# HGRN2 pair scores: two half-width products per tile against one full-width product on keys that ScalarE mixes, in a two-layer diffusion trunk

## The reference, cut to what matters

```python
def step(s, inp):                       # one chunk, one direction
    qc, kc, vc, lfc = inp
    cum = jnp.cumsum(lfc, axis=1)
    dec = jnp.exp(jnp.where(causal, cum[:, :, None] - cum[:, None], -jnp.inf))
    scores = jnp.sum(qc[:, :, None] * kc[:, None] * dec, axis=-1)
    o = jnp.einsum('btsh,bshv->bthv', scores, vc)
    o = o + jnp.einsum('bthk,bhkv->bthv', qc * jnp.exp(cum), s)
    ...
o_cf, s_cf = _hgrn2_chunkwise(q_c, kf_c, i_c, lf_c, s0)
o_lf, _ = _hgrn2_chunkwise(q_l, kf_l, i_l, lf_l, s_cf)
o_cb, s_cb = _hgrn2_chunkwise(rev(q_c), rev(kb_c), rev(i_c), rev(lb_c), s0)
o_lb, _ = _hgrn2_chunkwise(rev(q_l), rev(kb_l), rev(i_l), rev(lb_l), s_cb)
```

## Time and profile before

| | |
|---|---|
| Runs | 1993.79, 1994.34, 1997.75 us; median 1994.34 |
| The profiled execution | 1995.78 us; span 1994.0 us (its first to its last instruction), so 1.8 us lie outside the span |
| Busy, of the span | PE 1825.0 us (92%), DVE 1170.0 (59%), ACT 342.2 (17%), POOL 72.9 (4%) |
| Levels stage of layer 0 | about 346.1 to 434.6 us |
| Levels stage of layer 1 | about 1144.1 to 1196.4 us |
| Mean granted TensorE clock | 0.955 of 2.4 GHz |

### The profile page before, as it was taken

One profiled execution on the slowest core, in us unless ns is written; L12 is line 12 of the kernel. 1 busy time (PEld: TensorE's weight loads), 2 busy tenths in 40 slices (PEclk: granted clock), 3 DMA queues, 4 the chain that ended last, 5 costly groups with the idle time before them and its releaser, 6 DMA issues.

```text
span 1994.0 us, 34547 instructions
## 1 busy us (share of the span) xinstructions
PE 1825.0 (92%) x15227; PEld 1167.8 (59%) x15227; DVE 1170.0 (59%) x1387; ACT 342.2 (17%) x613; POOL 72.9 (4%) x60
## 2 busy tenths in 40 slices
PE   4999999986799999998999987699999999999997
PEld 1334556874344434344546665486877868677694
DVE  2021166783533222313223594599999999999996
ACT  2001054002422221212012403200000000100100
POOL 0023000000000000000050000000000000000000
PEclk9999999997899999999999997799999999999999
DMA  9631100001345544321212003399999999999999
GB/s 331 265 156 64 62 23 21 23 1 43 116 180 211 183 155 173 123 105 43 84 63 85 17 27 155 120 371 381 401 402 410 405 410 404 404 411 406 410 408 380
DMA packets 114980, 420.42 MB, mean 211 GB/s; under 512 B 14008, under 2 KB 20856, under 8 KB 108688
## 3 DMA queue, kind: packets, MB, share of 16 engines
q1 hardware_dynamic: 112784, 417.13, 53.8%
q10 hardware_dynamic: 2048, 1.02, 0.2%
HBM read 417.08 MB, written 1.05 MB: 210 GB/s over the span
## 4 chain that ended last, share of the span: by engine, by line
PE 78%; DVE 12%; issue 3%; DMA 3%; ACT 2%; DVEq 1%; POOLq 0%; SPq 0%; PEldq 0%; ACTq 0%; POOL 0%; PEld 0%
PE PS L1303 11%; PE PS L610 11%; PE PS L608 8%; PE PS L1590 6%; PE PS L1592 6%; PE PS L1593 6%; DVE ARENA L1708 6%; PE PS L1263 6%; PE PS L1612 5%; PE PS L1198 3%; PE PS L828 3%; PE PS L444 2%; PE PS L1091 2%; DMA ARENA<-in_ada_w 1%; PE PS L1570 1%
## 5 line engine op out<-in xcount | busy, mean ns | idle before, releaser
L1708 DVE TENSOR_TENSOR ARENA<-ARENA 128x2816 bf16<-128x2816 f32 (+1 forms) x192 | 584.1, 3085 | 21.6 <-DMA ARENA<-in_moe_w 19.7
L1590 PE MATMUL PS<-ARENA 128*128 128x96 bf16 x2816 | 377.2, 209 | 27.9 <-DVE ARENA L1708 15.8
L1593 PE MATMUL PS<-ARENA 128*128 128x96 bf16 x2816 | 376.7, 209 | 4.0 <-issue 4.0
L1592 PE MATMUL PS<-ARENA 128*128 128x96 bf16 x2816 | 376.9, 209 | 3.2 <-issue 3.1
L1590 PEld LDWEIGHTS PS<-ARENA 128*128 128x128 bf16 x2816 | 281.2, 100 | 39.3 <-issue 21.4
L1592 PEld LDWEIGHTS PS<-ARENA 128*128 128x128 bf16 x2816 | 281.2, 100 | 7.3 <-issue 7.2
L1593 PEld LDWEIGHTS PS<-ARENA 128*128 128x128 bf16 x2816 | 281.3, 100 | 4.1 <-issue 4.0
L610 PE MATMUL PS<-ARENA 128*128 128x512 f32 (+1 forms) x608 | 244.4, 542 | 2.3 <-ACTq L394 2.3
L1303 PE MATMUL PS<-ARENA 128*128 128x512 bf16 x1056 | 236.0, 384 | 2.4 <-DVE ARENA L1334 2.4
L1612 PE MATMUL PS<-ARENA 128*96 128x512 bf16 x1056 | 237.3, 384 | 0.0
L377 DVE TENSOR_TENSOR ARENA<-ARENA 128x4096 bf16<-128x4096 f32 (+1 forms) x26 | 91.4, 3522 | 201.9 <-ACT ARENA L371 201.9
(11 more groups left out here) (221 smaller groups left out, 1573.5 us busy)
## 6 DMA issues: line engine op xcount, KB each, us to landing
ARENA<-in_moe_w SPq DMA_DIRECT2D x136, 1408.0 KB, 11.4
ARENA<-in_moe_w SPq DMA_DIRECT2D x48, 1536.0 KB, 14.6
ARENA<-in_ada_w SPq DMA_DIRECT2D x24, 2048.0 KB, 9.6
ARENA<-in_ffn_w SPq DMA_DIRECT2D x15, 2048.0 KB, 7.6
ARENA<-in_w_in SPq DMA_DIRECT2D x12, 2048.0 KB, 8.0
ARENA<-in_moe_w SPq DMA_DIRECT2D x16, 1024.0 KB, 15.9
ARENA<-in_w_out SPq DMA_DIRECT2D x8, 1024.0 KB, 5.4
ARENA<-in_w_in SPq DMA_DIRECT2D x4, 1024.0 KB, 6.2
```

Of the source, the lines that this page charges most:

```text
L1590: pe.matmul(out, hi[:, f:f + P], HEH[:, k, :], start=k == 0 and b % 4 == 0, stop=False, skip_group_check=True)
L1592: pe.matmul(out, hi[:, f:f + P], HEL[:, k, :], start=False, stop=False, skip_group_check=True)
L1593: mm = pe.matmul(out, lo[:, f:f + P], HEH[:, k, :], start=False, stop=k == KC - 1, skip_group_check=True)
L1708: dve.tensor_tensor(WLO[q % NSLOT][:, 0:n], RAW[q % NSLOT][:, 0:n], WHI[q % NSLOT][:, 0:n], ALU.subtract).then_inc(S("m_lo"), 1)
```

## The change

`KE[d]` isn't the stationary matrix of a level any more. ScalarE copies the early half of each block from `KE[0]` and the late half from `KE[1]` into a new view `KEX` (two copies per pair and level, `act_cross_keys`), and PE makes one product per head and tile: `KEX` stationary, 128 query columns moving, into 128 columns of PSUM. The moving columns come from both query views: early-half queries from `QP[1]`, late-half queries from `QP[0]`. One access pattern with four dimensions reads them in the order of the tokens (`crossed_queries`); for it, the two query views change places, so that the step from `QP[1]` to `QP[0]` is positive. `KEX` lies at KiB 116 to 124, which nothing else uses in this stage. PE waits for both copies of its pair and level (semaphore `h{p}_keys`). A copy of level n >= 1 waits until PE is through with level n-1 of the pair (the old `KEX` has been read) and until DVE has ended the update of its direction. ScalarE's fetches of the output gate, which stood alone in its queue, now stand between the copies. The updates, the takes, the masks, level -1 and the products of the gate projection are as before.

```diff
--- before.py
+++ after.py
@@ -177,10 +177,11 @@
 
         ST = A(100, NH, 512)
         Q = A(16, NH, 512)
-        QP = [A(24, NH, 512), A(32, NH, 512)]
+        QP = [A(32, NH, 512), A(24, NH, 512)]
         KE = [A(40, NH, 512), A(48, NH, 512)]
         FG = [A(56, NH, 512), A(64, NH, 512)]
         TB = [A(108, 1024), A(112, 1024)]
+        KEX = A(116, NH, 512)
         SST = A(56, 3, 2, NH, P)
         KDT = A(68, 2, NH, P)
         V = A(72, NT, 512)
@@ -232,7 +233,7 @@
             "t_act": 4, "t_dve": 3, "dp_x": NT, "o_gated": 2 * NT,
             "o_added": 2 * NT, "out_mm": 2 * NT}
         for p in range(2):
-            in_layer0.update({f"h{p}_mm": 1 + len(LEVELS), f"h{p}_taken": 1 + len(LEVELS)})
+            in_layer0.update({f"h{p}_mm": 1 + len(LEVELS), f"h{p}_taken": 1 + len(LEVELS), f"h{p}_keys": 2 * len(LEVELS)})
             for d in range(2):
                 in_layer0.update({f"h{d}{p}_qp": 1, f"h{d}{p}_upd": 3 * len(LEVELS)})
         for step in ("s", "mx", "nb", "exp", "r", "ratio", "p", "pt", "at", "pv", "o"):
@@ -793,6 +794,28 @@
             new = totals(n_level + 1).rearrange("p (g b) -> p g b", g=2)
             eng.tensor_tensor(new, tv[:, :, :, 0], tv[:, :, :, 1], ALU.mult).then_inc(S(n + "upd"), 1)
 
+        SIDE = NH * 512
+
+        def crossed_queries(h, x, m):
+
+            a = 256 * 24 + 512 * h + P * x
+            v = ARENA[:, a:a + 2 * (SIDE + m)].rearrange("p (g w) -> p g w", g=2)[:, :, 0:P]
+            return v.rearrange("p g (b two m) -> p b g two m", two=2, m=m)[:, :, :, 0, :]
+
+        def act_cross_keys(act, L, n_level, p):
+
+            a, m = first_query(L), LEVELS[n_level]
+            if n_level:
+                act.wait_ge(S(f"h{p}_mm"), since(L, f"h{p}_mm") + n_level + 1)
+            for d in range(2):
+                if n_level:
+                    act.wait_ge(S(f"h{d}{p}_upd"), since(L, f"h{d}{p}_upd") + 3 * n_level)
+
+                def halves(v):
+                    return v[:, PAIRS[p], a:].rearrange("p g (b h m) -> p g b h m", h=2, m=m)[:, :, :, d, :]
+
+                act.activation(halves(KEX), halves(KE[d]), ACT.Copy).then_inc(S(f"h{p}_keys"), 1)
+
         def level_bank(n_level, p):
 
             return 2 * ((2 * (n_level + 1) + p) % 3)
@@ -808,6 +831,7 @@
                                 pe.wait_ge(S(n + "qp"), since(L, n + "qp") + 1)
                             else:
                                 pe.wait_ge(S(n + "upd"), since(L, n + "upd") + 3 * n_level)
+                        pe.wait_ge(S(f"h{p}_keys"), since(L, f"h{p}_keys") + 2 * n_level + 2)
                     at = 2 * (n_level + 1) + p
                     if at >= 3:
                         pe.wait_ge(S(f"h{1 - p}_taken"), since(L, f"h{1 - p}_taken") + (at - 3) // 2 + 1)
@@ -819,20 +843,22 @@
                                 pe.matmul(bank[:, c], KE[0][:, h, c], Q[:, h, c], start=True, stop=False)
                                 mm = pe.matmul(bank[:, c], KE[1][:, h, c], Q[:, h, c], start=False, stop=True)
                                 continue
-                            for d in range(2):
-                                late = 1 - d
-
-                                def halves(v):
-                                    return v.rearrange("p (b h m) -> p b h m", h=2, m=LEVELS[n_level])[:, :, late, :]
-
-                                mm = pe.matmul(halves(bank[:, c]), KE[d][:, h, c], halves(QP[d][:, h, c]), start=True, stop=True)
+                            mm = pe.matmul(bank[:, c], KEX[:, h, c], crossed_queries(h, x, LEVELS[n_level]), start=True, stop=True)
                     mm.then_inc(S(f"h{p}_mm"), 1)
                     w = KC * gate_units(L)
                     for step in range(w * at // 16, w * (at + 1) // 16):
                         pe_proj_fill(pe, L, KC * NT + step)
 
         def act_levels(act, L):
-            for j in range(gate_units(L)):
+            taken = 0
+            for n_level in range(len(LEVELS)):
+                for p in range(2):
+                    act_cross_keys(act, L, n_level, p)
+                    done = KC * gate_units(L) * (2 * n_level + p + 1) // 16 // KC
+                    while taken < done:
+                        act_proj_one(act, L, FIRST + NT + taken)
+                        taken += 1
+            for j in range(taken, gate_units(L)):
                 act_proj_one(act, L, FIRST + NT + j)
 
         def dve_take(dve, L, p, n_level):
```

## The result

| | before | changed |
|---|---|---|
| Median of the runs | 1994.07 us (8 runs) | 1998.91 us (8 runs) |
| Profiled execution | 1995.78 us | 2002.08 us |

What follows compares the result with a forecast made beforehand. The prediction took PE as the bound in layer 0's levels stage and DVE in layer 1's. Gains of 14.8 and 0.9 us, with copies costing 0, gave 1994.34 - 15.7 = 1978.6 us, range 1974.5 to 1984.5.

Steps and rivals of the forecast that it cites:

- Nothing else is moved: Outside the two levels stages: everything behind them, the expert stage included, only comes 15.7 us earlier.
- Bounds: Levels stages: PE bounds layer 0 at 5.29 us per position; DVE bounds layer 1, hiding PE's time.
- Term 1: New products in the levels stages: 0.110 us per record, so 1.76 us per layer 0 position instead of 3.52.
- the two ends given: Cost of a new product record with the crossed read: low bound 0.110 us, high bound 0.221 us.
- Term 2: DVE becomes layer 0's bound; its vanishing waits for products gain 14.8 us there and 0.9 us in layer 1.
- Term 3: ScalarE's new copies: 0.63 us each in layer 0, about 0.42 in layer 1, hidden, costing 0.
- 2.6 us to spare: Layer 0, pair 0: copy and products ready at 5.7 us of a level's 8.3, when DVE asks.
- Rival A: Level 0 alone dear: crossed read costs 0.221 us per record there; gain 11.7 us, total 1982.6 us; chance 0.08.
- B: Crossed read costs double at every level, positions as long as before; no gain, 1994.3 us; chance 0.04.
- D: Copies late at 3.5 times the estimate, ScalarE the bound; 4.2 us of gain lost, 1982.8 us; chance 0.04.
- C: Levels stages: PE's clock falls to half; 25 us lost in layer 0, about 8 in layer 1; 2027 us; chance 0.04.

Runs made afterwards that it cites:

- run 4: Changed kernel with 134 more met-wait instructions on PE and level 0's moving columns read from one query view, not crossed: 1979.49 us, ratio 0.9930 to the kernel before.
- run 8: Changed kernel with 134 more met-wait instructions on PE and each ScalarE copy made twice: 1982.34 us, ratio 0.9948 to the kernel before.
- run 1: Changed kernel with 134 more met-wait instructions on PE ahead of its first matmul: 1982.60 us, ratio 0.9932 to the kernel before.
- run 6: Changed kernel with PE's loop over the eight experts written out, no padding, other engines still looping: 1974.19 us, ratio 0.9897 to the kernel before.
- run 9: Changed kernel with 100 more met-wait instructions on PE ahead of its first matmul: 2027.48 us, ratio 1.0165 to the kernel before.
- run 3: Changed kernel with 60 more met-wait instructions on PE ahead of its first matmul: 2018.39 us, ratio 1.0121 to the kernel before.

## Why the prediction was wrong, step by step

- **"Nothing else is moved ... The expert stage, long as it is, starts from the end of layer 1's states and only shifts"** is the step that failed. What was moved was the code itself: 646 instructions fewer on PE ahead of a loop, so the loop's first instructions lie elsewhere in the pieces in which they are fetched. That gave back 19.4 us, more than the change had gained. The order listing had the count before the forecast was made (32 places fewer in each position of layer 0), and the page of the kernel before had the queue (q8, "instruction"); what was missing was to look at the stop at the branch in the loop and ask what it hangs on.
- Bounds (PE in layer 0, DVE in layer 1): right. The chain names DVE in layer 0 now.
- Term 1, the pace of the new products: 0.112 to 0.125 us from level 1 on in layer 0 and 0.12 to 0.13 in layer 1, but 0.166 at level 0, half way between the two ends given. Level 0 costs 1.4 us in layer 0 and 0.4 in layer 1 (run 4).
- Term 2, what DVE lets through: 14.8 + 0.9 forecast, 14.1 + 0.4 measured; the difference is mostly the dear level 0.
- Term 3, the copies: 0.65 and 0.42 us instead of 0.63 and 0.42; they cost nothing (run 8). PE does wait for them, 5.6 us in layer 0, which the sum with its 2.6 us to spare didn't have, but it has time for that.
- Rival A had the right mechanism at half its price: DVE's first wait stayed at 3.2 us instead of 4.0, the second at 0.4 instead of 1.3. B and D did not happen. C, the slower case, was about the clock: it stayed at 1.00 and 0.99 in the two stages. The kernel got slower for a reason that none of the rivals had.
- With the loop back at its old place the changed kernel takes 1982.6 us (run 1), 4.0 above the forecast and inside its range. Of these, 1.2 are the two stages' shortfall; the expert stage adds 0.8, the rest lies in the scatter of medians. That it is rival A's 1982.6 to the digit is chance: the two stages got 14.5 us shorter, not A's 11.7.

## What to carry to other kernels

When a change alters how many instructions an engine has ahead of a long loop, the loop's own time can change with it, by up to 45 us here for the same work, in a cycle of 256 instructions. Before an edit is judged by its total, compare the stages it doesn't touch; if one of them differs, with "issue" gaps at the same instruction of each pass, shift the loop with a few met waits and measure again. Where a loop on the bounding engine has few passes, writing it out removes the question.

## What the hardware showed that was not expected

- A taken branch in PE's queue costs 2.4 to 3.1 us in each pass of the kernel before while the weights keep the DMA engines at a share of 1.0, and PE has the second piece 5.1 to 5.5 us after it goes on, though PE then has nothing to do for up to 4.8 us. The Trainium skill ("Runtime: NRT & Kernel Launch", section Instruction fetch mechanics) says that a taken branch out of the window forces a fetch, and the stop at the branch agrees; written out, the loop lost it (run 6). The same section calls the crossing of a block's boundary mostly hidden. Here the measurement decides: later boundaries of a pass cost 0.2 to 1.3 us where they show at all, the first behind a branch up to 4.8. What it is that holds the second fetch back (the other transfers, or the order in which PE's sequencer asks) was not tried.
- PE's granted clock falls behind stops of this length: to 0.50 behind a stop of 2.6 us at the branch in the kernel before, while in the same pass of the changed kernel it was still at 1.00 there and fell only behind the second stop (0.67). Over the expert stage this costs little beside the stops themselves, 4.4 of the 46.6 us in run 9 and 8.3 of the 21.8 in run 3. Why it falls at one stop and not at another was not tried.
- A float32 product whose moving columns alternate between two views at every element takes 0.166 us per record instead of 0.111 (run 4); with two neighbours in a row (level 1) it takes 0.120 to 0.125 in layer 0, and from level 2 on 0.112 to 0.116.
